# A two-block transformer in fp32 on one core: the second block's layer loop written out, with other hand-overs at its two edges

## The chip, the cores and the metric

The kernel runs on one core of a Trainium2 chip. The metric is the device time of one execution, in microseconds. The core's engines run side by side and hand work over by semaphores: TensorE (PE) multiplies, VectorE (DVE) and ScalarE (ACT) work element by element, SyncE (SP) issues DMA transfers, and ACT issues some too. Each engine takes its own instructions in the order in which they are written.

## The reference

A sequence of 256 tokens with 1024 features goes through two blocks of two layers each. The first block (FFN, Fourier or retention mixer, FFN; modulated norms) ends in a final norm. The second block, which the change touches, is for each layer:

```
for l in range(DEPTH):
    f = _swiglu(_rmsnorm_2(h, ff1_norm_pre[l]), ff1_w_gate[l], ff1_w_up[l], ff1_w_down[l])
    h = h + 0.5 * _rmsnorm_2(f, ff1_norm_post[l])
    m = _hybrid_mixer(_rmsnorm_2(h, mix_norm_pre[l]), w_in[l], conv_w[l], ..., w_out[l])
    h = h + _rmsnorm_2(m, mix_norm_post[l])
    f = _swiglu(_rmsnorm_2(h, ff2_norm_pre[l]), ff2_w_gate[l], ff2_w_up[l], ff2_w_down[l])
    h = h + 0.5 * _rmsnorm_2(f, ff2_norm_post[l])
```

`_rmsnorm_2` divides by the root of the mean square over the features and multiplies by a gain; `_swiglu` is `(silu(h @ wg) * (h @ wu)) @ wd` with 2816 hidden features; the mixer holds a state-space part, a pooling part and attention. All is float32.

## The kernel before

**Layout.** Activations lie transposed: `h` holds 8 tiles of 128 features, each over the tokens (256 in the second block). A float32 product is made of three products in a reduced format: each operand is split into a high part and the rest (`u_hi`, `u_lo`; `w_hi`, `w_lo`; `g_hi`, `g_lo` for the hidden features of an FFN), and PE computes hi x hi, hi x lo and lo x hi (line 779).

**Weights.** Every matrix product (`Gemm`) is a row of units. A unit is a piece of weights, up to 4 tiles of 128 rows by 256 columns (512 KB). SP loads it into one of four slots of `raw` (`sp_gemm`, line 568) as soon as DVE has split the unit that lay there. ACT makes `w_hi` from it when PE has finished the unit of four places before (`split_hi`, line 581), and DVE makes `w_lo` (`split_lo`, line 587). The routine `stream` (line 590) writes the order of ACT and of DVE for a `Gemm`: at each unit u it first splits unit u + 4, and then evicts PSUM if u closes a pair of banks. If there is a next `Gemm` in the same list, its first four units are split within the stream of the current one (`follower`); if there is none, they are not.

**Stages.** `block1()` and `block2(l)` list the stages. Each engine walks through the lists and writes its own part. `first = block1()` is written out. `block2(l)` is written once per engine inside a hardware loop `Fori` over the two layers, so that semaphore counts are values in a register, computed from the layer. A layer is: gain, `up` (11 turns of four units), `down` (2 turns of six units), post norm, norm, the mixer's products and the mixer, `mix_out`, post norm, and again gain, `up`, `down`, post norm. Within `up` and longer products the turns after the first run in an inner `Fori`.

**The norm between two stages.** The last product's squares are summed by ACT and DVE, then over partitions by PE (lines 859, 862); ACT takes the root (841), DVE the reciprocal (850). `dve_post` (line 935) then walks over the eight tiles: `f_out` times `rstd` (943), and the result times the gain added to `h` (948). ACT makes `u_hi` of a tile from `h` and the next gain (893, `act_gain`), and DVE makes `u_lo` (900, `dve_gain_tile`), on which PE waits before the first product with that tile. The next stage's own `rstd` is applied later, behind the product: `up` has `norm_after`, so that a gate pair is evicted with the multiplication by `rstd` (696). When a gain stage follows in the same list, `dve_post` writes `dve_gain_tile` of tile k - 3 between the steps of tile k. This is so behind `mix_out`.

**The two edges.** At the end of the first block DVE multiplies tile by tile (lines 1771, 1772), all eight, and zeroes `poolw` (1774). ACT issues the load of `tables` (1696). At the start of each layer ACT splits the first four units of `up`, waits until all eight tiles are done (`post_ready`), issues four loads of `pool_w` (1708) and one of 8 columns of `w_in` into `dtw` (1709), and copies the layer's small vectors from `lvecs` to `lvec` (1711). Only then does `act_gain` scale the first tile. DVE splits one unit, waits for the copy and writes the gain tiles one behind the other (`dve_gain`). `tables`, `poolw` and `dtw` lie at the start of the memory that the first block's `g_hi` used; all are first read in the mixer.

Of the kernel before, what the change touches and what calls it, by code (L numbers as in the profile page):

```python
# [19 lines left out]
P = 128  # L20
D = 1024
DT = D // P
SEQ = 256
# [3 lines left out]
RING = 4  # L27
# [5 lines left out]
POOL_GROUPS = 4  # L33
ATTN_HEADS, ATTN_DH = 4, 64
LAYERS2 = 2
# [81 lines left out]
class Tally:  # L117
# [11 lines left out]

    def enter(self, layer, stages):  # L130

        self.start, self.per = dict(self.n), {}
        for s in stages:
            for k, v in s.counts().items():
                self.per[k] = self.per.get(k, 0) + v
        for k, v in self.per.items():
            self.n[k] = layer * v + self.start.get(k, 0)

    def leave(self, layers):
        self.n = dict(self.start)  # L140
        for k, v in self.per.items():
            self.n[k] = self[k] + layers * v
# [67 lines left out]
def build(nc, T):  # L210
# [27 lines left out]
    def block1():  # L238
# [51 lines left out]
        out.append(Stage("final", {"post": DT}))  # L290
        return out

    def block2(l):
        w = lambda name: T[name][l]
# [3 lines left out]
        def ffn(n, pre, post):  # L298
            gate, up = w(f"ff{n}_w_gate_2"), w(f"ff{n}_w_up_2")
            pick = lambda it, pair, k0, kt: rows((gate, up)[pair])[:, k0:k0 + kt, bass.ds(it * UCOLS, UCOLS)]  # L300
            return [Stage("gain", {"uhi": DT, "ulo": DT, "sq": 4, "sum": 2}, gain=pre),
# [4 lines left out]
                    stats(SEQ, "gemm", half=True), Stage("post", {"post": DT, "px": DT}, gain=post)]  # L306
        return ffn(1, "pre1", "post1") + [
            stats(SEQ, "post"), Stage("apply", {"xr": DT, "uhi": DT, "ulo": DT}, tokens=SEQ, gain="mix_pre"),
            Gemm("z", 1, [4, 4], in_turn(wi, 0), SEQ, evac="to_z", k_outer=True, waits="ulo"),
            Gemm("xbc", 2, [4, 4], in_turn(wi, 512), SEQ, evac="to_xbc"),  # L310
            Stage("conv", {}),
            Gemm("pool_v", 1, [4, 4], fixed((1544, 2312)), SEQ, mode="tokens", evac="to_pool_v"),
            Stage("steps", {}),
            Gemm("q_k", 1, [4, 4], fixed((1800, 2056)), SEQ, evac="to_q_k"),
            Stage("mixer", {"mix_lo": 3}),
            Gemm("mix_out", 2, [4, 4], in_turn(w("w_out_2")), SEQ, evac="store", waits="mix_lo", k_outer=True,
                 last_half_first=True),
            stats(SEQ, "gemm"), Stage("post", {"post": DT, "px": DT}, gain="mix_post")
# [7 lines left out]
    with ctx:  # L326
# [24 lines left out]
        lvec = sb("lvec", [P, LAYER_N])  # L351
# [28 lines left out]
        tab_spec = [("tables", [P, TWO_N], f32), ("poolw", [P, 2, P], f32), ("dtw", [P, 64], f32)]  # L380
# [26 lines left out]
        def lv(name, a=0, n=1):  # L407
            return lvec[:, LAYER_AT[name] + a:LAYER_AT[name] + a + n]
# [14 lines left out]
        lvec_copied = sem("lvec_copied")  # L423
# [100 lines left out]
        class Order:  # L524
# [5 lines left out]
            def enter(self, layer, per):  # L530
                self.first, self.per, self.n = self.n, per, layer * per + self.n
                self.k = 0

            def leave(self, layers):
                assert self.k == self.per, ("instructions of a layer in order", self.k)
                self.n = self.first + layers * self.per

            def link(self, ins):

                self.n = self.n + 1  # L540
# [1342 lines left out]
```

## Time and profile before

| | |
|---|---|
| device time of three runs | 3221.47, 3224.37, 3224.98 us; median 3224.37 |
| span of the profiled execution, first to last instruction | 3221.9 us |
| time of the profiled execution beside its span | not given separately; the median of the runs is 2.5 us above the span |
| TensorE matmul | busy 2935.3 us, 91% |
| TensorE weight load | 2633.6 us, 82% |
| DVE | 1701.1 us, 53% |
| ACT | 1283.5 us, 40% |
| DMA | 428.43 MB, mean 133 GB/s |
| mean granted TensorE clock | 0.953 of full |

Busy time is how long an engine had an instruction in work. Matmuls are pipelined, so their ends are modelled; their starts and the idle time ahead of them are the safer readings. The idle time ahead of an instruction stands in brackets, with the instruction that released it.

### The profile page before, as it was taken

The numbers are of one execution on the slowest core, as the hardware profiler recorded it, in microseconds if no ns is written. First come the engines' busy times: TensorE is split into PE (matmuls) and PEld (weight loads), VectorE is DVE, ScalarE is ACT, GpSimd is POOL, SyncE is SP. The second block draws the span as 40 slices with busy tenths as digits, with TensorE's granted clock in tenths as the row PEclk, the third lists the DMA queues.
The fourth block names the chain that finished last, engine by engine and source line by source line (L and its number), as shares of the span: only waits on it lengthen the run. The fifth ranks groups of instructions, "written<-read, shape, count | busy, mean of one in ns | idle before, by whom it ended". The sixth has DMA issues, their size and how long they took to land.

```text
span 3221.9 us, 47690 instructions
## 1 busy us (share of the span) xinstructions
PE 2935.3 (91%) x18444; PEld 2633.6 (82%) x18444; DVE 1701.1 (53%) x2287; ACT 1283.5 (40%) x1584; POOL 0.5 (0%) x7
## 2 busy tenths in 40 slices
PE   4999997899998999997997799898888989978898
PEld 3888886688886888886996799798868979977898
DVE  5554455455323553455237555665666656557664
ACT  5443334433223432334232444444434444444443
POOL 0000000000000000000000000000000000000000
PEclk8999998999999999998998899999898989989899
DMA  5454451155322453453340355565324646641464
GB/s 186 144 163 144 132 162 61 53 157 163 98 91 79 143 159 103 137 164 114 94 137 20 105 176 184 166 183 180 108 63 138 181 146 180 186 124 53 131 182 131
DMA packets 428460, 428.43 MB, mean 133 GB/s; under 512 B 16032, under 2 KB 426912, under 8 KB 428192
## 3 DMA queue, kind: packets, MB, share of 16 engines
q1 hardware_dynamic: 424736, 422.63, 43.1%
q10 hardware_dynamic: 3584, 3.90, 0.4%
q8 instruction: 92, 1.51, 0.2%
q14 instruction: 48, 0.39, 0.0%
HBM read 425.43 MB, written 1.05 MB: 132 GB/s over the span
## 4 chain that ended last, share of the span: by engine, by line
PE 86%; DVE 6%; ACT 4%; issue 2%; DMA 1%; ACTq 0%; DVEq 0%; SPq 0%
PE ps L779 72%; PE ps L767 4%; PE ps L753 3%; DVE rstd L850 1%; PE ps L859 1%; PE ps L862 1%; PE ps L1124 1%; DVE w_lo L587 1%; ACT w_hi L581 1%; ACT u_hi L877 1%; DMA raw<-in_w_mod 1%; PE ps L1008 1%; PE ps L1112 1%; DVE h L948 1%; ACT tmp L877 1%
## 5 line engine op out<-in xcount | busy, mean ns | idle before, releaser
L587 DVE TENSOR_TENSOR w_lo<-raw,w_hi 128x1024 fp32r<-128x1024 f32 (+1 forms) x816 | 973.8, 1203 | 1167.7 <-ACT w_hi L581 1151.6
L779 PE MATMUL ps<-u_hi,w_hi 128*128 128x256 f32 (+1 forms) x3648 | 1184.7, 325 | 116.5 <-DVE u_lo L926 50.9
L581 ACT ACTIVATE w_hi<-raw 128x1024 fp32r<-128x1024 f32 (+1 forms) x816 | 837.7, 1038 | 1128.3 <-PE ps L779 1038.2
L779 PE MATMUL ps<-u_lo,w_hi 128*128 128x256 f32 (+1 forms) x3648 | 1173.7, 322 | 0.0
L779 PE MATMUL ps<-u_hi,w_lo 128*128 128x256 f32 (+1 forms) x3648 | 1173.6, 322 | 0.0
L779 PEld LDWEIGHTS ps<-u_hi,w_hi 128*128 128x128 f32 x3648 | 708.8, 194 | 182.9 <-issue 53.1
L779 PEld LDWEIGHTS ps<-u_hi,w_lo 128*128 128x128 f32 x3648 | 708.9, 194 | 48.7
L779 PEld LDWEIGHTS ps<-u_lo,w_hi 128*128 128x128 f32 x3648 | 710.2, 195 | 44.8
L779 PE MATMUL ps<-g_hi,w_hi 128*128 128x256 f32 (+1 forms) x1408 | 451.4, 321 | 0.0
L779 PE MATMUL ps<-g_hi,w_lo 128*128 128x256 f32 (+1 forms) x1408 | 451.2, 320 | 0.0
L779 PE MATMUL ps<-g_lo,w_hi 128*128 128x256 f32 (+1 forms) x1408 | 451.2, 320 | 0.0
L779 PEld LDWEIGHTS ps<-g_hi,w_lo 128*128 128x128 f32 x1408 | 264.1, 188 | 24.3
L779 PEld LDWEIGHTS ps<-g_hi,w_hi 128*128 128x128 f32 x1408 | 264.2, 188 | 22.3
L779 PEld LDWEIGHTS ps<-g_lo,w_hi 128*128 128x128 f32 x1408 | 264.2, 188 | 21.9
L753 PE MATMUL ps<-w_hi,cond_cols 128*128 128x256 f32 x576 | 146.4, 287 | 30.2 <-DVE turned L627 15.9
L660 ACT ACTIVATE g_hi<-tmp 128x512 f32 (+3 forms) x88 | 69.8, 793 | 229.1 <-DVE tmp L708 229.1
L753 PE MATMUL ps<-w_lo,cond_cols 128*128 128x256 f32 x576 | 145.5, 286 | 0.0
L753 PEld LDWEIGHTS ps<-w_hi,cond_cols 128*128 128x128 f32 x576 | 111.5, 194 | 36.2 <-issue 26.5
L713 DVE TENSOR_TENSOR g_lo<-tmp,g_hi 128x512 f32 (+3 forms) x88 | 78.5, 892 | 90.9 <-ACT g_hi L660 90.9
L753 PEld LDWEIGHTS ps<-w_lo,cond_cols 128*128 128x128 f32 x576 | 111.4, 193 | 5.0
L859 PE MATMUL ps<-acc,ones 128*128 128x256 f32 (+1 forms) x76 | 38.3, 644 | 67.7 <-DVE acc L827 45.0
L819 ACT ACTIVATE tmp<-h 128x512 f32<-128x512 f32 (+1 forms) x57 | 42.3, 742 | 139.3 <-DVE h L727 65.9
(222 smaller groups left out, 2041.1 us busy)
## 6 DMA issues: line engine op xcount, KB each, us to landing
raw<-in_ffn_w_in SPq DMA_DIRECT2D x176, 512.0 KB, 3.5
raw<-in_w_mod SPq DMA_DIRECT2D x144, 512.0 KB, 4.5
raw<-in_ff_w_gate SPq DMA_DIRECT2D x88, 512.0 KB, 4.0
raw<-in_ff_w_up SPq DMA_DIRECT2D x88, 512.0 KB, 4.2
raw<-in_ffn_w_out SPq DMA_DIRECT2D x64, 512.0 KB, 3.4
raw<-in_ff_w_down SPq DMA_DIRECT2D x64, 512.0 KB, 4.0
raw<-in_ret_w_in SPq DMA_DIRECT2D x48, 512.0 KB, 3.7
raw<-in_w_in SPq DMA_DIRECT2D x40, 512.0 KB, 3.7
```

The lines of the kernel that those rows point to most:

```text
L581: act.activation(w_hi[:, slot, 0:cols], raw[:, slot, 0:cols], ACT.Copy).then_inc(hi_ready, 1)
L587: dve.tensor_tensor(w_lo[:, slot, 0:cols], raw[:, slot, 0:cols], w_hi[:, slot, 0:cols].bitcast(f32), ALU.subtract).then_inc(lo_ready, 1)
L660: act.activation(hi[:, bass.ds((it + g.first) * 2, 2), 0:g.tokens], tmp2[:, :, 0:g.tokens], ACT.Copy).then_inc(g_hi_ready, 1)
L713: dve.tensor_tensor(lo[:, two, 0:g.tokens], tmp2[:, :, 0:g.tokens], hi[:, two, 0:g.tokens].bitcast(f32), ALU.subtract).then_inc(g_lo_ready, 1)
L753: ins = pe.matmul(ps[:, 4 + pair % 2, 0:UCOLS], cond_cols[:, 4 * (k0 + k):4 * (k0 + k) + P], w[:, slot, k * UCOLS:(k + 1) * UCOLS], start= ...
L767: ins = pe.matmul(out, a, w[:, slot, cols], start=begins and k == 0 and n == 0 and tb % 2 == 0, stop=final and k == kt - 1 and n == 2, ski ...
L779: ins = pe.matmul(out, w[:, slot, cols], a, start=begins and k == 0 and n == 0, stop=final and k == kt - 1 and n == 2)
L819: act.activation(out[:, :, 0:n], source[:, 2 * m:2 * m + 2, 0:n], ACT.Square).then_inc(squares_ready, 1)
L850: dve.reciprocal(rstd[:, 0:n], rstd[:, 0:n]).then_inc(rstd_ready, 1)
L859: pe.matmul(ps[:, STAT, 0:n], ones[:, :], acc[:, i, 0:n], start=i == 0, stop=False)
L862: ins = pe.matmul(ps[:, STAT, 0:n], ones[:, :], tmp1[:, i, 0:n], start=False, stop=i == 1)
L877: ins = act.activation(out[:, tok], tmp2[:, k % 2, tok], ACT.Identity, scale=coef[:, g.more["piece"], k, s:s + 1], bias=mod[:, g.more["pie ...
```

## The change

The layer loop over the second block is replaced by one list of both layers' stages, written out for each engine, so semaphore counts there are constants except in the inner loops. `follower` now sees over both edges (`whole` for the first block's products, `second` for the layers'). At the first edge `dve_final` zeroes `poolw`, then handles norm and gain tiles interleaved as `dve_post` does; at the layer edge `dve_post` finds the gain stage behind it. `lvec`, its copy and its semaphore are gone; `lv(l, ...)` reads `lvecs`. `poolw` and `dtw` hold both layers' data. They and `tables` are loaded once, by SP, in `sp_tables`, between the last tile of the first layer's first `up` and the first tile of its `down`.

```
-        tab_spec = [("tables", [P, TWO_N], f32), ("poolw", [P, 2, P], f32), ("dtw", [P, 64], f32)]
+        tab_spec = [("tables", [P, TWO_N], f32), ("poolw", [P, 2 * LAYERS2, P], f32), ("dtw", [P, LAYERS2, 64], f32)]
...
+        def sp_tables(sp):
+            sp.wait_ge(poolw_zeroed, 1)
+            sp.dma_start(tables[:, :], T["tables2"]).then_inc(tables_landed, 16)
+            for l in range(LAYERS2):
+                sp.dma_start(dtw[:, l, :].rearrange("p (k n) -> p k n", n=8),
+                             rows(T["w_in_2"][l])[:, :, 1536:1544]).then_inc(dtw_landed, 16)
+                for g in range(POOL_GROUPS):
+                    r = slice((g % 2) * 64, (g % 2 + 1) * 64)
+                    sp.dma_start(poolw[r, 2 * l + g // 2, r], T["pool_w_2"][l, g]).then_inc(poolw_landed, 16)
...
+        def dve_final(dve, t, gain):
+            dve.memset(poolw[:, :, :], 0.0).then_inc(poolw_zeroed, 1)
+            dve.wait_ge(lvec_landed, 16)
+            if begun(t["stat"]):
+                dve.wait_ge(rstd_ready, t["stat"])
+            for k in range(DT + 3):
+                if k < DT:
+                    if begun(k - 1):
+                        dve.wait_ge(post_ready, k - 1)
+                    dve.tensor_tensor(tmp2[:, k % 2, 0:SEQ], h[:, k, 0:SEQ], rstd[:, 0:SEQ], ALU.mult
+                                      ).then_inc(post_scaled_ready, 1)
+                if 0 < k <= DT:
+                    dve.wait_ge(post_scaled_ready, k)
+                    dve.tensor_scalar(h[:, k - 1, 0:SEQ], tmp2[:, (k - 1) % 2, 0:SEQ], vecs("final_g", k - 1), None,
+                                      ALU.mult).then_inc(post_ready, 1)
+                if k >= 3:
+                    dve_gain_tile(dve, gain, t, k - 3)
...
+        second = [stage for l in range(LAYERS2) for stage in block2(l)]
+        whole = first + second
...
@@ @block.sync
-            with sp.Fori(0, LAYERS2) as l:
-                stages = block2(l)
...
+            for g in second:
+                if isinstance(g, Gemm):
+                    sp_gemm(sp, g, t)
+                t.add(g)
+                if g is follower(second, -1):
+                    sp_tables(sp)
...
@@ @block.scalar
-                    stream(act, g, t, follower(first, j), split_hi, act_evacuate)
+                    stream(act, g, t, follower(whole, j), split_hi, act_evacuate)
...
-                act.dma_start(tables[:, :], T["tables2"]).then_inc(tables_landed, 16)
-            with act.Fori(0, LAYERS2) as l:
-                for u in range(RING):
-                    split_hi(act, follower(stages, -1), t, 0, u)
-                act.wait_ge(lvec_landed, 16)
-                act.wait_ge(poolw_zeroed, 1)
-                act.wait_ge(post_ready, t["post"])
-                for g in range(POOL_GROUPS):
-                    act.dma_start(poolw[r, g // 2, r], T["pool_w_2"][l, g]).then_inc(poolw_landed, 16)
-                act.dma_start(dtw[:, :].rearrange("p (k n) -> p k n", n=8), ...
-                act.activation(lvec[:, :], lvecs[:, bass.ds(l * LAYER_N, LAYER_N)], ACT.Copy
-                               ).then_inc(lvec_copied, 1)
+            act.wait_ge(lvec_landed, 16)
+            for j, g in enumerate(second):
+                if isinstance(g, Gemm):
+                    stream(act, g, t, follower(second, j), split_hi, act_evacuate)
...
@@ @block.vector
-                split_lo(dve, up, t, 0, 0)
-                dve.wait_ge(lvec_copied, l + 1)
-                        if j == 0:
-                            dve_gain(dve, g, t, {3: [1], 7: [2, 3]}, up)
+                    behind = second[j + 1] if j + 1 < len(second) and second[j + 1].kind == "gain" else None
+                    dve_post(dve, g, t, behind)
```

## Rows read from the trace of the kernel before

**Rows 1.** The page's chain of waits, share by engine.
```profile
PE 86%; DVE 6%; ACT 4%; issue 2%; DMA 1%; ACTq 0%; DVEq 0%; SPq 0%
```

**Rows 2.** Groups by line and form, PE: count | busy us, mean ns | idle before, releasers.
```profile
L779 PE MATMUL ps<-u_hi,w_hi 128*128 128x256 f32 x2464 | 716.1, 291 | 78.2 <-DVE u_lo L900 39.1 <-DVE u_lo L926 23.8 <-ACT tmp L651 5.4
...
L779 PE MATMUL ps<-u_hi,w_lo 128*128 128x256 f32 x2464 | 707.6, 287 | 0.0
...
L779 PE MATMUL ps<-g_hi,w_lo 128*128 128x256 f32 x880 | 242.9, 276 | 0.0
```

**Rows 3.** Timeline, first edge: start us, duration us, instruction [idle before <-releaser].
```profile
2035.36 0.28 PE L779 MATMUL ps<-g_hi,w_lo 128*128 128x256 f32 x1
...
2038.94 1.75 DVE L850 RECIPROCAL rstd<-rstd 128x256 f32<-128x256 f32 x1 [2.39 <-ACT rstd L841]
...
2046.60 0.27 DVE L1774 MEMSET poolw<- 128x256 f32 x1
...
2051.99 0.58 PE L779 MATMUL ps<-u_hi,w_hi 128*128 128x256 f32 x1 [13.58 <-DVE u_lo L900]
...
2066.81 0.68 DVE L696 TENSOR_TENSOR tmp<-ps,rstd 128x512 f32<-128x512 f32 x1
```

**Rows 4.** Timeline, layer edge.
```profile
2621.30 0.28 PE L779 MATMUL ps<-g_hi,w_lo 128*128 128x256 f32 x1
...
2624.77 1.75 DVE L850 RECIPROCAL rstd<-rstd 128x256 f32<-128x256 f32 x1 [2.47 <-ACT rstd L841]
...
2633.49 2.47 ACTq L1708 DMA_DIRECT2D poolw<-in_pool_w  x4
...
2638.22 0.58 PE L779 MATMUL ps<-u_hi,w_hi 128*128 128x256 f32 x1 [14.00 <-DVE u_lo L900]
...
2653.42 0.68 DVE L696 TENSOR_TENSOR tmp<-ps,rstd 128x512 f32<-128x512 f32 x1
```

**Rows 5.** Timeline, inside the layer, behind mix_out.
```profile
2414.92 0.28 PE L779 MATMUL ps<-u_hi,w_lo 128*128 128x256 f32 x1
...
2422.53 1.75 DVE L850 RECIPROCAL rstd<-rstd 128x256 f32<-128x256 f32 x1 [3.78 <-ACT rstd L841]
...
2427.72 0.58 PE L779 MATMUL ps<-u_hi,w_hi 128*128 128x256 f32 x1 [5.74 <-DVE u_lo L900]
...
2444.72 0.68 DVE L696 TENSOR_TENSOR tmp<-ps,rstd 128x512 f32<-128x512 f32 x1
```

**Rows 6.** Timeline and one window, behind the first layer's first down.
```profile
2243.40 0.28 PE L779 MATMUL ps<-g_hi,w_lo 128*128 128x256 f32 x1
...
2244.80 1.23 DVE L587 TENSOR_TENSOR w_lo<-raw,w_hi 128x1024 fp32r<-128x1024 f32 x1 [0.81 <-ACT w_hi L581]
...
2250.83 1.75 DVE L850 RECIPROCAL rstd<-rstd 128x256 f32<-128x256 f32 x1 [3.60 <-ACT rstd L841]
...
core 0: us, PE busy (x) PEld busy (x) DVE busy (x) ACT busy (x) POOL busy (x), PEclk, DMA share, GB/s
2243.40:2250.83 7.43, 3.88 (x11) 2.60 (x9) 3.02 (x4) 2.16 (x3) 0.00 (x0) 0.77 0.70 210
```

**Rows 7.** Timeline, first up to first down: SP, ACT, PE.
```profile
2163.16 0.37 SPq L568 DMA_DIRECT2D raw<-in_ff_w_up  x1
...
2167.56 0.37 SPq L568 DMA_DIRECT2D raw<-in_ff_w_down  x1
...
2176.75 1.04 ACT L581 ACTIVATE w_hi<-raw 128x1024 fp32r<-128x1024 f32 x1
...
2183.66 0.29 PE L779 MATMUL ps<-g_hi,w_hi 128*128 128x256 f32 x1
```

**Rows 8.** DMA issues: count, KB each, median us from issue to landing.
```profile
tables<-in_tables ACTq DMA_DIRECT2D x1, 1920.0 KB, 7.2
...
poolw<-in_pool_w ACTq DMA_DIRECT2D x8, 16.0 KB, 2.0
```

**Rows 9.** Timeline, nine linked small instructions, layer loop and first block.
```profile
2329.91 1.85 DVE L977 SCALAR_TENSOR_TENSOR small<-small 128x16 f32<-128x16 f32 x9
...
1516.86 1.77 DVE L977 SCALAR_TENSOR_TENSOR lgam<-lgam 128x8 f32<-128x8 f32 x9
```

More of the change, by code:

```diff
@@ L128, in add @@
             self.n[k] = self[k] + v
[L130 to L142, printed above, removed]
 def loop(eng, a, b, body):
@@ L289, in block1 @@
         out.append(stats(SEQ, "gemm"))
-        out.append(Stage("final", {"post": DT}))
+        out.append(Stage("final", {"post": DT, "px": DT}))
         return out
     def block2(l):
+        of_layer = lambda kind, counts: Stage(kind, counts, layer=l)
         w = lambda name: T[name][l]
@@ L350, in build @@
         lvecs = sb("lvecs", [P, LAYERS2 * LAYER_N])
-        lvec = sb("lvec", [P, LAYER_N])
         mod = sb("mod", [P, 3, 24, 2])
@@ L528, in __init__ @@
                 self.eng, self.sem, self.n = eng, sem, 0
[L530 to L536, printed above, removed]
             def link(self, ins):
                 self.n = self.n + 1
-                self.k = self.k + 1 if hasattr(self, "k") else 0
                 ins.then_inc(self.sem, 1)
@@ L880, in act_apply_tile @@
                 else:
-                    ins = act.activation(out[:, 0:n], tmp2[:, k % 2, 0:n], ACT.Copy, scale=lv(g.more["gain"], k))
+                    ins = act.activation(out[:, 0:n], tmp2[:, k % 2, 0:n], ACT.Copy, scale=lv(*g.more["gain"], k))
             ins.then_inc(u_hi_ready, 1)
@@ L892, in act_gain @@
                     act.wait_ge(post_ready, t["post"] - DT + k + 1)
-                act.activation(u_hi[:, k, 0:SEQ], h[:, k, 0:SEQ], ACT.Copy, scale=lv(g.more["gain"], k)
+                act.activation(u_hi[:, k, 0:SEQ], h[:, k, 0:SEQ], ACT.Copy, scale=lv(*g.more["gain"], k)
                                ).then_inc(u_hi_ready, 1)
@@ L899, in dve_gain_tile @@
             dve.wait_ge(u_hi_ready, t["uhi"] + k + 1)
-            dve.scalar_tensor_tensor(u_lo[:, k, 0:SEQ], h[:, k, 0:SEQ], lv(g.more["gain"], k),
+            dve.scalar_tensor_tensor(u_lo[:, k, 0:SEQ], h[:, k, 0:SEQ], lv(*g.more["gain"], k),
                                      u_hi[:, k, 0:SEQ].bitcast(f32), ALU.mult, ALU.subtract
@@ L904, in dve_gain_tile @@
                 dve_add_squares(dve, SEQ, k // 2, t)
-        def dve_gain(dve, g, t, units_after, gemm):
-            for k in range(DT):
-                dve_gain_tile(dve, g, t, k)
-                for u in units_after.get(k, []):
-                    split_lo(dve, gemm, t, 0, u)
         def dve_scaled(dve, g, t, k):
@@ L1748, in _ @@
                 if isinstance(g, Gemm):
-                    stream(dve, g, t, follower(first, j), split_lo, dve_evacuate, dve_turn_rows)
+                    stream(dve, g, t, follower(whole, j), split_lo, dve_evacuate, dve_turn_rows)
                 elif g.kind == "squares":
@@ new lines, in _ @@
+                    dve_final(dve, t, second[0])
+                t.add(g)
+            for j, g in enumerate(second):
+                if isinstance(g, Gemm):
+                    if g.norm_after:
+                        dve_stats(dve, stats(g.tokens, "gemm"), t)
+                    stream(dve, g, t, follower(second, j), split_lo, dve_evacuate, dve_turn_rows)
+                elif g.kind == "stats":
+                    dve_stats(dve, g, t)
+                elif g.kind == "apply":
+                    dve_apply(dve, g, t)
+                elif g.kind == "post":
+                    behind = second[j + 1] if j + 1 < len(second) and second[j + 1].kind == "gain" else None
+                    dve_post(dve, g, t, behind)
+                elif g.kind == "conv":
+                    dve_conv(dve, t, g.more["layer"], order)
+                elif g.kind == "steps":
+                    dve_steps(dve, g.more["layer"], order)
+                elif g.kind == "mixer":
+                    dve_mixer(dve, g.more["layer"], order)
+                t.add(g)
```

156 lines of the change are left out of this document (51 added, 105 removed).

## The prediction

> **What bounds the kernel now.** The chain of waits comes first: TensorE (PE) holds 86% of it, VectorE (DVE) 6% [rows 1]. A change to the other engines counts only where PE stands still. The groups by line and form come next: behind its 2464 first matmuls on `u_hi` stand 78.2 us of idle time, of which 39.1 end on `u_lo L900` [rows 2]. These waits are few and long, so the timeline is the third view. PE stops for 13.58 us between the first block and the second [rows 3] and for 14.00 us between the two layers [rows 4]. These are the two edges that the change rewrites. Inside a layer the same norm already hands over tile by tile: behind `mix_out`, PE waits 5.74 us for the same first `u_lo` tile [rows 5]. That seam and the one behind the first `down` [rows 6] show what the edges become, because they run the code that the edges get.
>
> I measure each edge between two points that lie on PE's path: the start of the last matmul of the old stage, and the first `L696`, which evicts the first gate pair of `up`. From there the loops of `up` run alike. Before: first edge 2066.81 - 2035.36 = 31.45 us [rows 3], layer edge 2653.42 - 2621.30 = 32.12 us [rows 4].
>
> **Hand-over tile by tile (removes).** Today DVE finishes all eight tiles of the norm, then ScalarE (ACT) issues four `pool_w` loads (2.47 us [rows 4]), one `dtw` load and the copy of `lvec`, and only then scales the first tile. In the change DVE interleaves the gain tiles three behind the norm, and ACT has no loads there. From the start of the reciprocal to the first `L696` that is 27.87 us at the first edge [rows 3], 28.65 us at the layer edge [rows 4] and 22.19 us inside the layer [rows 5]. Gains: 5.68 and 6.46 us, 12.14 us together. The branch back of the layer loop lies inside the 28.65 us and goes with it.
>
> **Look-ahead over the edge (adds, on the path).** `stream` of the last `down` now has a follower, so ACT and DVE split the first four units of `up` inside it. The split of the fourth unit needs the slot that the last unit of `down` frees. It therefore starts when PE is done, and in both queues it stands ahead of the last eviction: behind it wait the squares sum, the copy out of PSUM, the last squares and the stat matmuls. Today the edges have none of this: last matmul to reciprocal is 2038.94 - 2035.36 = 3.58 us [rows 3] and 3.47 us [rows 4]. The first `down` of the layer, which has a follower, shows it: ACT's split, then DVE's (1.23 us from 2244.80, though the last matmul began at 2243.40), and the reciprocal at 2250.83, 7.43 us after that matmul [rows 6]. `mix_out` needs 7.61 us [rows 5]. TensorE's granted clock over those 7.43 us is 0.77 on average, so part of the stretch ran at the 1.2 GHz level; the stall ahead of the stat matmuls is part of the price. I take 7.43, as the stage before both edges is a `down`.
>
> Layer edge after: 7.43 + 22.19 = 29.62 us, against 32.12: **-2.50 us**. First edge after: 7.43 + 22.19, plus 0.11 because its eviction with residual is slower (3.58 against 3.47), plus the zeroing of `poolw`. That memset is twice as wide now and stands between the reciprocal and the first norm tile. The half-width one took 0.27 us [rows 3]; the wide one lies between that and 0.54, I take 0.4. Sum 30.13 us against 31.45: **-1.32 us**. That the final norm only multiplies where the post norm also adds to `h` I leave at nothing. The two edges together: **-3.8 us**. With 7.61 for 7.43 at both it would be -3.5, and if the look-ahead delayed nothing it would be 12.14 - 0.4 = -11.7. The measured seam is the nearest row, and I keep -11.7 for the range.
>
> **Tables on the weight queue (moves).** SyncE (SP) issues `tables`, two `dtw` and eight `poolw` loads right behind the last tile of the first `up`, ahead of the first tile of `down`. SP's last `up` tile goes out at 2163.16 and the first `down` tile at 2167.56 [rows 7]. ACT's four `poolw` issues took 2.47 us [rows 4], 0.62 each; eleven such are 6.8 us, so the first `down` tile leaves at about 2170.3, 2.8 us late. Its data stand behind the transfers: 7.2 us for the 1920 KB of `tables` [rows 8], at that rate 1.9 us for the `up` tile ahead of it and 1.9 us for its own 512 KB, and for ten small loads, mostly overlapped, an estimated 2 us. It lands at 2163.2 + 13.0 = 2176.2. ACT wants it at 2176.75, and PE only at 2183.66 [rows 7], after a split by ACT and one by DVE that take about 2.3 us. What hides the loads is thus PE's 20 us of work on tiles that came before them. **Cost 0**; without that cover it would be the 9.2 us of other loads that stand ahead of the tile. From above: if each of the ten small loads held the queue for its full 2.0 us [rows 8], the tile would land at 2163.2 + 11.0 + 20 = 2194.2 and PE would stand for 2194.2 + 2.3 - 2183.66 = 12.8 us. Below zero nothing is to be had here: the loads that leave ACT are already counted at the edges.
>
> **Layer loop written out, per-layer constants, `lvec` gone.** Waits against a register become waits against a constant, and small operands come from `lvecs` in place. The nine linked instructions of `L977` took 1.85 us inside the layer loop, on 16 columns, and 1.77 us in the first block, with constants and on 8 columns [rows 9]. At most 0.08 us in nine waits could be the register, and I expect none. PE waits in a row of its own only at the seams above. Cost and gain **0**. As PE covers the rest of both layers, a hidden saving on ACT or DVE moves nothing; only the edges count.
>
> **Sum.** Edges -3.8, tables 0, loop 0. Against the profiled span of 3221.9 us that is 3218.1 us. The median of the runs is 3224.37 us, 2.5 us above that span, and the same difference makes **3220.6 us**, or -0.12%. About 0.2% (6.4 us) is what a measurement of this kernel can tell from no change, so I forecast no change that counts. Own range of this case: -2 to -6 us, 3218 to 3222.5.
>
> **Rivals.**
> - *The look-ahead delays nothing.* If the last splits fell in time ahead of the eviction, the edges would give 11.7 us: 3212.7 us. For it: the reciprocal-to-`L696` rows alone promise that much. Against: both seams with a follower show over 7.4 us from last matmul to reciprocal, both without one under 3.6 [rows 3 to 6]. Chance 0.12.
> - *The tables starve the ring (slower).* Small loads held one behind another in the SP queue make the first `down` tile late for PE. It decides once the tile lands after 2183.66 - 2.3 = 2181.4, 5.2 us later than I take, and makes the kernel slower than before 3.8 us beyond that. At the bound worked out above: -3.8 + 12.8, 3233.4 us. For it: the loads stood in ACT's queue, in a stretch in which PE was idle; now they stand in the queue of the tiles, at full demand. Against: the slack. Chance 0.06. By the Trainium skill (DMA: Bandwidth & Descriptors, "Queues, rings and completion order") a DMA engine takes the descriptors of one queue's ring in order, but changes between the rings of different queues packet by packet. That speaks against the move: on ACT's ring the weights could pass the tables, on SP's they can't. No row here shows two such loads on one ring.
> - *Placement (slower).* `lvec` (456 bytes) lay ahead of the `g` tiles, and `poolw` and `dtw` grow ahead of the second block's. PE's 256-column matmuls on `g` tiles take 276 ns, those on `u` tiles 287 [rows 2]. Only the latter run in part at the half clock, behind the seams; I take 7 of the 11 ns as pace. Nothing in the profile says why, so it may hang on the address. If `g` fell to the pace of `u`, that is 3 x 880 matmuls x 7 ns = 18.5 us: 3220.6 + 18.5 = 3239.1 us. Against: the tiles of the first and the second block lie at different addresses and keep one mean. Chance 0.07. The same cause could speed up others; with what else I don't see, 0.05 for a gain of some 10 us.
> - *The edge doesn't pipeline.* If the gain tiles waited for the whole norm, as now, each edge would lose ACT's loads (2.47 us and up) and pay 7.43 - 3.47 = 3.96 for the look-ahead: up to 3.0 us for both, 3227 us at most. The order of the code inside the layer speaks against it. Chance 0.04.
>
> **How the numbers follow.** The forecast has 0.66. Faster by over 0.2%: 0.12 + 0.05 and 0.09 of my own case, where both edges give more than I count: 0.26. Slower by over 0.2%: 0.06 + 0.07 less what stays small: 0.11. Within: 0.63. The range takes in the first rival and the spread of the runs before (3221.47 to 3224.98), and leaves out the two slow rivals and the far end of the fast one: 3212 to 3226.5.
>
> **What would show it.** Right: at both edges a split of 1.2 us on DVE directly ahead of the last eviction, the reciprocal 7.3 to 7.7 us after the last matmul, PE's wait for the first `u_lo` near 5.7 us instead of 14, and reciprocal to first `L696` near 22.2 us. ACT's wait for a raw tile at the start of the first `down` under 1 us and no PE wait there. `g` matmuls still at 276 ns. Wrong: the reciprocal under 5 us after the last matmul, PE idle at the start of the first `down`, other means for L779, or a stage away from the edges that changes its length by more than 1 us.

## The result, and the profile after

The changed kernel takes 3236.3 us (median of 7 runs, 3233.6 to 3239.4), the kernel before 3224.4 us beside it: ratio 1.0035, 95% interval 1.0025 to 1.0044. I had forecast 3220.6 us. The change makes the kernel slower by 12 us, and the time lies near the rival "placement", which I had given 0.07.

The page of the changed kernel shows the same bound as [rows 1]. Its groups by line and form answer to [rows 2]; L767 is now the line of the GEMM matmuls.

```profile
PE 86%; DVE 7%; ACT 4%; issue 2%; DMA 1%; SPq 0%; ACTq 0%; DVEq 0%
```

```profile
L767 PE MATMUL ps<-u_hi,w_hi 128*128 128x256 f32 x2464 | 718.5, 292 | 62.3 <-DVE u_lo L908 23.8 <-DVE u_lo L888 22.9 <-ACT tmp L639 5.1
...
L767 PE MATMUL ps<-u_hi,w_lo 128*128 128x256 f32 x2464 | 709.0, 288 | 0.0
...
L767 PE MATMUL ps<-g_hi,w_lo 128*128 128x256 f32 x880 | 247.3, 281 | 0.0
```

The idle time ahead of `u_hi` fell from 78.2 to 62.3 us: the change did what it says, though not all of that reaches the total, as the look-ahead puts part of it back ahead of the statistics. But the matmuls on `g` with 256 columns went from 276 to 281 ns, three groups of 880, 242.9 to 247.3 us each: 13.2 us. These run back to back, so here that is time on the path. One down stage shows it by its starts. The rows give count, duration min/median/max, and the first and last start; first the kernel before, then the changed one, the same stage.

```profile
L779 PE MATMUL ps<-g_hi,w_hi x176: 276/276/286, 1975.6 to 2035.1; 128*128 128x256 f32 x176
```

```profile
L767 PE MATMUL ps<-g_hi,w_hi x176: 276/281/286, 1981.0 to 2043.1; 128*128 128x256 f32 x176
```

59.5 us became 62.1 us: 113.4 ns from start to start became 118.3 (59.5 / 525 and 62.1 / 525: the row holds every third matmul, and from its first to its last start there are 525 steps). All five down stages with 256 columns show the same, 5 x 2.6 = 13.0 us.

The first edge, for [rows 3]:

```profile
2043.35 0.28 PE L767 MATMUL ps<-g_hi,w_lo 128*128 128x256 f32 x1
...
2044.82 1.23 DVE L575 TENSOR_TENSOR w_lo<-raw,w_hi 128x1024 fp32r<-128x1024 f32 x1 [0.90 <-ACT w_hi L569]
2045.96 0.68 DVE L815 TENSOR_TENSOR acc<-acc,tmp 128x512 f32<-128x512 f32 x1
...
2050.43 1.75 DVE L838 RECIPROCAL rstd<-rstd 128x256 f32<-128x256 f32 x1 [3.00 <-ACT rstd L829]
2052.24 0.48 DVE L939 MEMSET poolw<- 128x512 f32 x1
...
2055.58 0.55 PE L767 MATMUL ps<-u_hi,w_hi 128*128 128x256 f32 x1 [5.69 <-DVE u_lo L888]
...
2072.31 0.68 DVE L684 TENSOR_TENSOR tmp<-ps,rstd 128x512 f32<-128x512 f32 x1
```

And the layer edge, for [rows 4]:

```profile
2629.94 0.28 PE L767 MATMUL ps<-g_hi,w_lo 128*128 128x256 f32 x1
...
2631.41 1.23 DVE L575 TENSOR_TENSOR w_lo<-raw,w_hi 128x1024 fp32r<-128x1024 f32 x1 [0.90 <-ACT w_hi L569]
...
2637.67 1.75 DVE L838 RECIPROCAL rstd<-rstd 128x256 f32<-128x256 f32 x1 [3.84 <-ACT rstd L829]
...
2642.86 0.55 PE L767 MATMUL ps<-u_hi,w_hi 128*128 128x256 f32 x1 [5.73 <-DVE u_lo L888]
...
2659.74 0.68 DVE L684 TENSOR_TENSOR tmp<-ps,rstd 128x512 f32<-128x512 f32 x1
```

From the last matmul to the first gate eviction: 2072.31 - 2043.35 = 28.96 us (before 31.45) and 2659.74 - 2629.94 = 29.80 us (before 32.12). The edges give 4.8 us, and I had forecast 3.8. Each step of the forecast is there: DVE's split of 1.2 us ahead of the eviction, the reciprocal 7.08 and 7.73 us after the last matmul, 5.7 us of wait for the first `u_lo` tile.

A third difference lies far from the change, at 632 us. Windows of both kernels, the column after POOL being the granted clock:

```profile
632.00:638.00 6.00, 4.70 (x19) 3.57 (x20) 3.97 (x7) 6.00 (x14) 0.00 (x0) 0.99 0.00 0
```

```profile
632.00:638.00 6.00, 5.53 (x12) 3.94 (x13) 3.98 (x8) 6.00 (x13) 0.00 (x0) 0.50 0.00 0
```

In the changed kernel TensorE stays at 1.2 GHz (a granted clock of 0.50) some 6 us longer behind the same waits. From the norm's reciprocal at 621 us to the next one at 1033 us the kernel before takes 1033.57 - 621.35 = 412.22 us, the changed one 1036.86 - 621.21 = 415.65: 3.4 us more. The sum of the three, 13.0 - 4.8 + 3.4 = 11.6 us, is nearly all of the 12.4 us between the two profiled spans.

### The profile page after: what moved, and what is told of

It reads as the page before. It is cut to its first block, busy times and chain, and to the rows that moved or that the text cites. A ratio compares the mean times of both kernels' runs of the same rounds, so it can differ in the third digit from the quotient of the medians.

```text
span 3234.3 us, 46336 instructions
## 1 busy us (share of the span) xinstructions
PE 2957.5 (91%) x18444; PEld 2652.8 (82%) x18444; DVE 1699.8 (53%) x2287; ACT 1285.1 (40%) x1582; POOL 0.5 (0%) x7
## 3 DMA queue, kind: packets, MB, share of 16 engines
q1 hardware_dynamic: 427600, 424.79, 43.4%
## 4 chain that ended last, share of the span: by engine, by line
PE 86%; DVE 7%; ACT 4%; issue 2%; DMA 1%; SPq 0%; ACTq 0%; DVEq 0%
PE ps L767 73%; PE ps L741 3%; PE ps L755 3%; DVE rstd L838 1%; PE ps L1125 1%; ACT w_hi L569 1%; PE ps L850 1%; DVE w_lo L575 1%; PE ps L847 1%; ACT u_hi L865 1%; DMA raw<-in_w_mod 1%; PE ps L1009 1%; ACT tmp L865 1%; DVE tmp L925 1%; DVE h L930 1%
## 5 line engine op out<-in xcount | busy, mean ns | idle before, releaser
L767 PE MATMUL ps<-u_hi,w_hi 128*128 128x256 f32 (+1 forms) x3648 | 1188.8, 326 | 99.8 <-DVE u_lo L908 50.2
L767 PE MATMUL ps<-u_lo,w_hi 128*128 128x256 f32 (+1 forms) x3648 | 1177.3, 323 | 0.0
L767 PE MATMUL ps<-u_hi,w_lo 128*128 128x256 f32 (+1 forms) x3648 | 1176.7, 323 | 0.0
L767 PEld LDWEIGHTS ps<-u_hi,w_hi 128*128 128x128 f32 x3648 | 710.9, 195 | 169.3 <-issue 89.8
L767 PEld LDWEIGHTS ps<-u_hi,w_lo 128*128 128x128 f32 x3648 | 711.5, 195 | 48.4
L767 PEld LDWEIGHTS ps<-u_lo,w_hi 128*128 128x128 f32 x3648 | 712.9, 195 | 44.8
L767 PE MATMUL ps<-g_lo,w_hi 128*128 128x256 f32 (+1 forms) x1408 | 456.2, 324 | 0.0
L767 PE MATMUL ps<-g_hi,w_lo 128*128 128x256 f32 (+1 forms) x1408 | 456.1, 324 | 0.0
L767 PE MATMUL ps<-g_hi,w_hi 128*128 128x256 f32 (+1 forms) x1408 | 456.1, 324 | 0.0
L767 PEld LDWEIGHTS ps<-g_hi,w_lo 128*128 128x128 f32 x1408 | 265.1, 188 | 23.7
L767 PEld LDWEIGHTS ps<-g_lo,w_hi 128*128 128x128 f32 x1408 | 265.1, 188 | 21.9
L767 PEld LDWEIGHTS ps<-g_hi,w_hi 128*128 128x128 f32 x1408 | 265.1, 188 | 21.8
```

The costliest lines, as they stand in the source:

```text
L767: ins = pe.matmul(out, w[:, slot, cols], a, start=begins and k == 0 and n == 0, stop=final and k == kt - 1 and n == 2)
```

## The experiments

**a1_align: the old addresses back.** A byte address below is that in a partition's memory, as the compiler assigned it. The `g` tiles started at 133952 before and start at 133472 in the changed kernel, because `lvec` (480 bytes with padding) is gone. The second block's `g` tiles stood at 150592 and stand at 151392: there the growth of `poolw` and `dtw`, 1024 + 256 = 1280 bytes, comes on top, a multiple of 256.

```
         lvecs = sb("lvecs", [P, LAYERS2 * LAYER_N])
+        pad = sb("pad", [P, 120])
```

> The changed kernel with a dead buffer of 480 bytes per partition where lvec lay, nothing else. The g tiles of both blocks then start 64 bytes past a multiple of 128 again, as in the kernel before; in the changed kernel they start 96 past. Placement theory: the starts of the 256-column matmuls on g tiles stand 113.4 ns apart again instead of 118.3 in all five such down stages, 5 x 528 x 4.9 ns = 12.9 us, so 3236.3 - 12.9 = 3223.4 us, and 3220 where TensorE gets the full clock in the seam at 628 us as early as in the profile of before. Rival, the written-out loop or the look-ahead is what costs: 118.3 ns stay, 3236 us.

Measured: 3217.9 us (12 runs), ratio to the kernel before 0.9983, interval 0.9974 to 0.9991. The same stage as above:

```profile
L768 PE MATMUL ps<-g_hi,w_hi x176: 276/276/286, 1975.1 to 2034.6; 128*128 128x256 f32 x176
```

59.5 us again, and in all five stages. 480 dead bytes take 18.4 us off the medians; 13.0 of them are this pace, and another 3.4 between the two profiles is the late clock at 632 us, which this profile doesn't have. Without the placement the change is faster than the kernel before, by 6.9 us, more than my 3.8.

**a2_before_pad32: the placement alone.**

```
         eps = sb("eps", [P, 2])
+        pad = sb("pad", [P, 8])
```

> The kernel before with 32 dead bytes per partition ahead of the g tiles, nothing else: they start 96 bytes past a multiple of 128 instead of 64. Placement theory: 118.3 ns between the 256-column matmuls on g tiles instead of 113.4, no other stage moves, 3224.4 + 12.9 = 3237.3 us. Rival, placement costs nothing and the difference is in the change's code: 113.4 ns stay, 3224 us.

Measured: 3240.5 us (5 runs), ratio 1.0049, interval 1.0036 to 1.0062. The same stage:

```profile
L780 PE MATMUL ps<-g_hi,w_hi x176: 277/281/285, 1978.0 to 2040.2; 128*128 128x256 f32 x176
```

62.2 us, and all five stages run so. Nothing of the change is in this kernel, and it is slower than the changed one by about what the edges give. (Of its 15.7 us, 13 are this pace; the rest is not broken down.) Together with a1_align this shows the cause from both sides.

**a3_late_split: the fourth split off the path.**

```
-                    elif nxt is not None:
+                    elif nxt is not None and not (g.squares and u == g.units - 1):
                         split(eng, nxt, t_next, 0, v - g.units)
...
+            split_late(split_hi)      # ACT: behind the root in act_stats
...
+            split_late(split)         # DVE: first thing in stream of the next GEMM
```

> a1_align, and in addition the fourth look-ahead split of every stage that ends in a residual or a store is taken out of the stage: ACT issues it behind the root of the statistics, DVE ahead of the next GEMM's loop. That holds at both rewritten edges and at nine seams inside the blocks. My step (the fourth split stands ahead of the last eviction and costs 7.43 - 3.5 = 3.9 us): reciprocal 3.5 us after the last matmul at each such seam, 11 seams x up to 3.9 us = up to 43 us less than a1_align; with 512 tokens less, so 20 to 43 us. Rival, the split is hidden and the 7.43 us are the eviction's own: no change against a1_align. Rival, the fourth unit now comes late for TensorE: the reciprocals are early and the time comes back as idle time ahead of the fourth unit.

Measured: 3191.7 us (4 runs), ratio 0.9893, interval 0.9879 to 0.9908: 26 us under a1_align. The first edge of its trace:

```profile
2020.31 1.23 DVE L576 TENSOR_TENSOR w_lo<-raw,w_hi 128x1024 fp32r<-128x1024 f32 x1 [0.82 <-ACT w_hi L570]
...
2020.88 0.28 PE L777 MATMUL ps<-g_hi,w_lo 128*128 128x256 f32 x1
...
2025.17 1.05 ACT L570 ACTIVATE w_hi<-raw 128x1024 fp32r<-128x1024 f32 x1
2025.31 1.75 DVE L849 RECIPROCAL rstd<-rstd 128x256 f32<-128x256 f32 x1 [2.39 <-ACT rstd L839]
```

The fourth split is now the ACT row at 2025.17, beside DVE's reciprocal. The reciprocal comes 4.43 us after the last matmul, against 2042.29 - 2034.88 = 7.41 in a1_align; the third split still ends behind the last matmul, the likely reason why it is not 3.5. So the look-ahead's price, 7.43 - 3.5, was read rightly, and 3.0 of the 3.9 us can be had back up to the reciprocal. Of that TensorE loses some behind the seam: at four seams it waits some 0.6 us for a split. The 26 us are 2.4 us for each of the 11 seams.

**b3_edge_late: the first rival of the prediction made true.** As a3_late_split, at the two rewritten edges alone (`nxt.more.get("edge")` in the condition).

> a1_align with the late fourth split at the two rewritten edges alone. This is the rival of the prediction in which the look-ahead delays nothing, made true: against a1_align 2 x 3.3 us less (a3_late_split lost 3.32 us at the first edge and 1.85 at the second between the marks of the two profiles), 3217.9 - 5.2 to 6.6 = 3211 to 3213 us. Rival, at the edges the splits are covered and all of a3's 26 us come from the seams inside the blocks: 3218.

Measured: 3217.9 us (11 runs), ratio 0.9979, interval 0.9970 to 0.9988; a1_align had 0.9983. The forecast was too high. It counted 3.32 and 1.85 us for the two edges of a3_late_split, but between this document's two points they took 2048.35 - 2020.88 = 27.47 and 2625.22 - 2597.51 = 27.71 us, 3.5 under a1_align in all. Here too, the two edges take 2065.31 - 2038.56 = 26.75 and 2647.17 - 2618.75 = 28.42 us, against 29.70 and 28.97 in a1_align, so 3.5 us come out at them, not 5.2 to 6.6, while the runs of either kernel spread over 8 to 11 us. No difference is shown. At the layer edge only 0.55 us are left, though the first product starts 9.44 us after the last matmul and not 12.42. Two windows of 4 us, each from 4 us after that product, first in a1_align, then here, show where part of it goes:

```profile
2633.56:2637.56 4.00, 4.00 (x29) 4.00 (x29) 3.15 (x8) 2.15 (x4) 0.00 (x0) 0.79 0.00 0
```

```profile
2632.19:2636.19 4.00, 4.00 (x21) 4.00 (x21) 3.15 (x8) 2.15 (x4) 0.00 (x0) 0.50 0.00 0
```

The granted clock stays at its lower level longer, 21 matmuls start in the window and not 29, and behind it TensorE waits 0.56 us for a split. With one profile of each kernel, how much of this is the edit's and how much the execution's is not shown.

**b2_after_again: is the late clock the change's?** The changed kernel, unchanged.

> The changed kernel once more, unchanged, for a second profile. Its first profile lost 3.4 us against the kernel before in the seam at 628 us, where the full clock came at 638.6 instead of 632.5 us with the same work ahead of it. Theory, that is the lot of an execution: the second profile has the full clock near 632.5 at that place, or another such place moves. Rival, it belongs to the changed kernel: 638.6 again.

Measured: 3234.0 us, one run. The same place:

```profile
632.00:638.00 6.00, 6.00 (x18) 4.75 (x19) 3.60 (x6) 6.00 (x13) 0.00 (x0) 0.63 0.00 0
```

This profile is late again, by 3.4 us from reciprocal to reciprocal (1034.46 - 618.87 = 415.59 us). But b3_edge_late, whose instructions up to 2000 us are a1_align's, has 0.61 in this window and 3.3 us too, while a1_align has 1.00 and nothing. So it is not tied to the placement or to the change's code; whether the changed kernel draws it more often isn't settled. The Trainium skill (TensorE: Matmul & The Clock Gate, Part 1) says of the rise of the clock that it is "run-variable"; these traces agree.

**d2_tables_gpsimd: what the tables cost on SP.** In the changed kernel SP's row of the first up to the first down, for [rows 7] (start, duration, instruction, count):

```profile
2166.30 2.65 SPq L545 DMA_DIRECT2D raw<-in_ff_w_up  x2
2169.16 0.35 SPq L553 DMA_DIRECT2D tables<-in_tables  x1
2169.57 0.43 SPq L555 DMA_DIRECT2D dtw<-in_w_in  x1
2170.03 5.78 SPq L559 DMA_DIRECT2D poolw<-in_pool_w  x4
2175.85 0.59 SPq L555 DMA_DIRECT2D dtw<-in_w_in  x1
2176.48 2.95 SPq L559 DMA_DIRECT2D poolw<-in_pool_w  x4
2179.47 12.58 SPq L545 DMA_DIRECT2D raw<-in_ff_w_down  x8
```

Eleven issues take 10.3 us, not my 6.8. ACT then waits 0.88 and 0.43 us for raw tiles, and TensorE not at all:

```profile
2183.14 1.06 ACT L569 ACTIVATE w_hi<-raw 128x1024 fp32r<-128x1024 f32 x1 [0.88 <-DMA raw<-in_ff_w_down]
2184.64 1.06 ACT L569 ACTIVATE w_hi<-raw 128x1024 fp32r<-128x1024 f32 x1 [0.43 <-DMA raw<-in_ff_w_down]
```

The edit of the run, on a1_align:

```
-                if g is follower(second, -1):
-                    sp_tables(sp)
...
+            sp_tables(pool)
```

> a1_align with the eleven loads of tables, dtw and poolw issued by GpSimd as soon as poolw is zeroed, at the edge, and none on SP. It tests the prediction's step that the tables cost nothing on the weight queue. My step (hidden by 20 us of TensorE's work): no change against a1_align, 3218 us, and the first down of the layer starts no earlier. Rival, the tables do hold the weight ring back: up to 12.8 us less, 3205 us. If they come to lie in the way of the first up's weights at the edge, it is slower than a1_align.

Measured: 3220.2 us (11 runs), ratio 0.9987, interval 0.9978 to 0.9996. No gain is shown (a1_align had 0.9983): the step "cost 0" holds.

**a4_bench and b1_bench_addresses: matmuls alone, on zeros.**

```
for j, (w, x) in enumerate(((wh, hi), (wh, lo), (wl, hi))):
    ins = mm(out, at(w + w0, P), at(x + x0, n), k == 0 and j == 0, k == 3 and j == 2)
```

> Matmuls alone, on zeros, no work of the kernel in it: runs of 96 in the kernel's pattern (weights hi, hi, lo; moving hi, lo, hi), one line of code for each placement. The moving tiles start 0, 32, 64 or 96 bytes (and 16, 48, 80) past a multiple of 128, with 256 or 512 columns; the weights at 0, 32 or 64. Theory, the start of the moving tile sets the pace: with 256 columns 120 ns at 0 (as the u tiles, which start at 0), 118.3 at 96, 113.4 at 64; with 512 columns 226.7 at 0 and 233 at 64 and 96. Rival, something else in the stages makes the pace (the transfers and the other engines beside them, the distance of the two halves): one spacing for all placements of a size.

Measured: 117 to 119 ns from start to start for all seven starts of the moving tile with 256 columns; 231 to 233 with 512. The theory, that the tile's own start sets the pace, fell. In this bench the high and the low halves happened to stand 128 bytes apart modulo 256, so no line had one distance for all its matmuls; the second bench has.

> Matmuls alone again, on zeros, no work of the kernel in it, but every operand at the byte address that it has in the kernel (one buffer over the partition), with the kernel's loops over the two halves of the columns and four inner tiles; one line of code for each placement. In the first bench no start of the moving tile gave the 113.4 ns of the g tiles: 117.8 to 118.8 for all. Theory 1, what counts is where the two moving halves and the two weight halves stand relative to each other: the addresses of the g tiles before give 113.4, those after 118.3, those of the u tiles 120, with nothing running beside; moving u by 64 bytes shows whether it can be had for u too. Theory 2, the other engines and the transfers make the difference: all near 118.

Measured, one row for each placement (96 matmuls, first and last start):

```profile
L72 PE MATMUL ps<-X x96: 281/281/281, 105.0 to 116.2; 128*128 128x256 f32 x96
...
L74 PE MATMUL ps<-X x96: 280/283/283, 127.7 to 139.1; 128*128 128x256 f32 x96
L75 PE MATMUL ps<-X x96: 276/276/286, 139.2 to 150.0; 128*128 128x256 f32 x96
L76 PE MATMUL ps<-X x96: 277/280/285, 150.1 to 161.3; 128*128 128x256 f32 x96
...
L86 PE MATMUL ps<-X x96: 279/279/283, 262.8 to 274.0; 128*128 128x256 f32 x96
...
L92 PE MATMUL ps<-X x96: 279/284/285, 331.3 to 342.7; 128*128 128x256 f32 x96
L93 PE MATMUL ps<-X x96: 276/276/284, 342.8 to 353.6; 128*128 128x256 f32 x96
...
L98 PE MATMUL ps<-X x96: 389/389/397, 399.2 to 420.7; 128*128 128x512 f32 x96
L99 PE MATMUL ps<-X x96: 394/394/394, 421.0 to 443.1; 128*128 128x512 f32 x96
...
L107 PE MATMUL ps<-X x96: 276/276/285, 555.0 to 565.8; 128*128 128x256 f32 x96
```

The span over 95 is the pace, good to 1 ns, as starts are given to 0.1 us. Write d for the start of the moving tile less that of the weights, modulo 256. L74 has the addresses of `u` (d = 0): 120.0 ns. L75 has those of the second block's `g` before (d = -64): 113.7. L76 has those after (d = -32): 117.9. L86 is `u` 64 bytes further (d = 64): 117.9; L92 is the old `g` with the weights 64 further (d = 128): 120.0. L93 is `u` with the weights 64 further (d = -64): 113.7. The other distances stand in the last section. So no other engine and no transfer is needed for the difference, and both operands count. One pair doesn't fit a fixed pace for each distance: L72 and L107 have the same addresses, those of the first block's `g` before (d = -64), and took 117.9 and 113.7 ns. f2_u192_again comes back to this. With 512 columns the order turns round: d = 0 (L98) 226.3 ns, d = -64 (L99) 232.6.

**e1_after_pad32: the rule tried on g.**

```
         eps = sb("eps", [P, 2])
+        pad = sb("pad", [P, 8])
```

> The changed kernel with 32 dead bytes per partition ahead of the g tiles, for its trace: g then starts where u does, at distance 0 from the weights modulo 256. If the distance is what counts, the 256-column matmuls on g tiles start 120 ns apart, as those on u do, neither 118.3 as in the changed kernel nor 113.4 as in the kernel before; 5 x 528 x 1.7 ns = 4.5 us more than the changed kernel, 3238 to 3241 us. Rival, any place but the old one gives 118.3; or a round multiple of 128 gives the fast pace back, 3223 us.

Measured: 3229.5 us, one run. A stage with 256 columns, and one with 512:

```profile
L768 PE MATMUL ps<-g_hi,w_hi x176: 283/283/283, 1969.9 to 2032.9; 128*128 128x256 f32 x176
...
L768 PE MATMUL ps<-g_hi,w_hi x176: 389/389/389, 897.7 to 1016.7; 128*128 128x512 f32 x176
```

63.0 / 525 = 120.0 ns in all five, as the rule says. I forgot its other half for the sum: with 512 columns the pace went from 233 (the changed kernel: 903.7 to 1026.2, 122.5 us) to 227 ns (119.0 us), 3.5 us in this stage. The first of the three such stages became shorter by 2.5 us (144.1 to 141.6), the third by about as much, some 8.5 us together. 3236.3 + 4.5 - 8.5 = 3232.3 us; the one run took 3229.5, and the 2.8 us between are not explained.

**c1_weights64, c2_u64, d1_u192, f1_all_distances: using it.** All on a3_late_split. The first moves the weights by 64 bytes; the others move `u` from the retention norm on, by a view that starts 16 or 48 columns further. In c2 the buffers also grow by 128 bytes, so that the two halves of `u` stand at +64 and -64; in d1 and f1 they grow by 256, and both halves stand at -64. f1 moves wide `g` tiles too, and zeroes `poolw` ahead of the reciprocal:

```
+        wpad = sb("wpad", [P, 16])                    # c1
...
+            u_hi.first = u_lo.first = 16 if (...) else 0   # c2; d1: 48
...
+            u_hi.first = u_lo.first = g_hi.first = g_lo.first = 48 if (...) else 0   # f1
-        g_hi, g_lo = overlay([("g_hi", [P, FT, NTOK], f32r), ...])
+        g_hi, g_lo = [Moved(None, t, FT) for t in overlay([("g_hi", [P, FT * NTOK + 64], f32r), ...])]
```

> a3_late_split with 64 dead bytes per partition ahead of the two weight halves. They and the g tiles behind them move by 64 bytes, u stays: g keeps its distance to the weights, u changes it from 0 to 64 (mod 128). In the second bench the addresses of u gave 120.0 ns with 256 columns and 113.7 once the weights stood 64 bytes further; with 512 columns 226.3 and 233.7. Theory, the distance between the moving tile and the weights (mod 128) sets the pace: the stages on u with 256 columns fall from 120.0 to 113.5 ns between starts, (3 x 2464 + 960) x 6.4 ns = 54 us, where TensorE never waits at half pace; the stages on u with 512 columns rise from 226.8 to 233, 3 x 1184 x 6.5 ns = 23 us; g stays at 113.4. 3191.7 - 54 + 23 = 3161 us, and 3175 if a third of the gain lies beside waits. Rival, the start address of the moving tile alone counts: u stays at 120, g goes to another pace, 3192 to 3215 us.

> a3_late_split with u 64 bytes further from the retention norm on, that is for nearly all stages with 256 columns, and at its old place for those with 512; the weights stay. Same theory as for c1_weights64 without its loss: 3191.7 - 50 = 3142 us, 3155 if part lies beside waits; starts 113.5 ns apart in the GEMMs on u from 1500 us on. In the bench u moved by 64 gave 117.9 instead of 113.7, so half the gain, 3170, is possible too. Rival as there: no change, 3192.

> c2_u64 with u moved by 192 bytes instead of 64, and the two halves of u 65 x 256 bytes long, so that both stand alike. The g tiles of the kernel before stand 64 bytes short of the weights, counted modulo 256, and so do all lines of the second bench with 113.7 ns, while a distance of 0 gave 120, 128 gave 118.9 to 120, and 64, 32 and 96 gave 117.9. Theory, the distance modulo 256 counts and 192 (that is -64) is the fast one: u goes from 120.0 to 113.4 ns in every stage with 256 columns from 1480 us on, which c2_u64 reached only in the token stages (its two halves stood at +64 and -64): 3191.7 - (7392 + 960) x 6.6 ns = 3137 us, 3150 if part lies beside waits. Rival, the distance is only half of it and a stage falls into one pace or another by chance, as c1_weights64 showed with the same distances (113.4 ns in some stages, 117.8 in others): 3155 to 3180 us.

> d1_u192 with the wide g tiles treated as u is: at distance 0 from the weights (modulo 256) in the three down stages with 512 columns, at -64 in the last one with 256; the second block's g stays at -64; and the zeroing of poolw stands ahead of the reciprocal instead of behind it. Theory: in e1_after_pad32 the 512-column matmuls on g went from 233 to 227 ns at distance 0, so 3 x 528 x 3 x 6.5 / 3 ns = 10 us, and 0.5 us for the zeroing: 3165 - 10.5 = 3155 us, clearly under d1_u192. Rival, the 512-column stages gain nothing in this setting, or stages with 256 columns fall to 117.8 ns by chance as often as before and cover it: 3155 to 3165 us without order.

Measured: c1 3182.7 us (0.9842, 0.9816 to 0.9869), c2 3180.7 (0.9857, 0.9841 to 0.9874), d1 3165.1 (0.9811, 0.9797 to 0.9824), f1 3157.4 (0.9786, 0.9768 to 0.9804). Each is faster than a3_late_split, by the ratios, and c1, c2 and d1 give less than the rule promised. d1 gained 27 us of the 55 counted, 37 in its profile: some stages ran at 117.8 ns though they stand at d = -64. In c2 the low half of `u` stands at d = 128 in the early stages, and these got slower besides: 192 matmuls with 512 columns, back to back, took 44.6 us where a3_late_split took 43.4. f1 has the 512-column stage below at 227 ns (119.0 us for 525 steps) and the lowest median of the study, 67 us under the kernel before, though its interval and d1's overlap:

```profile
L791 PE MATMUL ps<-g_hi,w_hi x176: 389/389/390, 891.1 to 1010.1; 128*128 128x512 f32 x176
```

**f2_u192_again: what picks the pace at d = -64.**

> d1_u192 unchanged, for a second profile: in the first one the five down stages with 256 columns, all at distance -64, ran at 117.8, 113.6, 113.3, 113.3 and 113.3 ns, and the retention stages on u at 117.8. Theory, addresses fix the possible paces, and which of 113.4 or 117.8 a stage takes is fixed by the program's order: the same stages are slow again. Rival, it is drawn in each execution: other stages, or none or all.

Measured: 3169.0 us, one run. The first layer's second down stage, in d1_u192 and in its repeat:

```profile
L790 PE MATMUL ps<-g_hi,w_hi x176: 276/276/276, 2518.3 to 2577.8; 128*128 128x256 f32 x176
```

```profile
L790 PE MATMUL ps<-g_hi,w_hi x176: 280/281/282, 2521.6 to 2583.4; 128*128 128x256 f32 x176
```

59.5 and 61.8 us: the same program at the same addresses, 113.4 ns in one execution and 117.8 in the other. The up and down stages of one run of matmuls mostly share the pace. So at d = -64 the pace is partly drawn in the execution, as L72 and L107 of the bench had it within one. What it hangs on stays open. Where `u` stands at d = 0, every down stage at d = -64 ran at 113.4 ns: 25 of 25, in the profiles of before, a1, a3, b3 and d2.

## Why the prediction was wrong, point by point

**The step that failed** is "Layer loop written out, per-layer constants, `lvec` gone", whose cost and gain the sum put at 0. Taking away a buffer of 456 bytes moved the `g` tiles from d = -64 to d = -32, and that slowed 2640 matmuls by 4.9 ns each: 13.0 us, shown from both sides by a1_align and a2_before_pad32. The prediction had this as a rival, with the right place and sign. It gave 3239.1 us against 3236.3 measured, but that closeness is partly luck. It took 7 ns, the way to the pace of `u` (120.0 - 113.4 = 6.6 by the starts), and `g` went to 118.3 only. With 4.9 ns it would have said 3233.5, and the late clock of 3.4 us, which it didn't have, makes up the difference. Its chance of 0.07 was too low. I argued against it that the tiles of both blocks "lie at different addresses and keep one mean". They do, but at the same distance from the weights modulo 256, and I didn't work the addresses out, though the sizes of the buffers were all in the code.

**The edges** were read rightly: 4.8 us against 3.8 (a1_align: 4.9). Both parts are there, the hand-over tile by tile and the look-ahead that takes most of it back. The first edge gave more (2.5 against 1.3). Its reciprocal came 7.08 us after the last matmul where the sum had 7.54 (7.43 + 0.11). From the reciprocal on it took 21.88 us where the sum had 22.59: the zeroing took 0.48 us, not 0.4, so the other 21.40 us are 0.79 less than [rows 5]. That the final norm only multiplies, which I left at nothing, may be why; no run shows it. At the layer edge it is 22.07 us against 22.19.

**The look-ahead's price** was right in kind: a3_late_split moves one split per seam and gains 26 us. The rival that it delays nothing is refuted by the traces. That the same price stood at nine more seams, I did not say. Of the 26 us of a3_late_split 3.5 come out at the two edges and the other 22 or so at these, against the 4.8 us that the whole change gives at both edges.

**The tables** cost nothing, as forecast, but with less room: the first down tile leaves SP at 2179.5, 10.3 us after the first table, and TensorE takes up that down stage at 2189.1. I put its landing at 2176.2; ACT got it at 2183.14, 3.7 us after its issue, and the median of such tiles is 3.5. So ACT's two short waits come from the late issue. The rule of the Trainium skill that I set against the move (order within a ring) had no part in the tile's delay: `tables`, issued at 2169.16, took 9.0 us to land and was through before the tile left SP. The `dtw` loads on that ring took 6.0 us to land (median) where they took 2.7 on ACT's before, which agrees with the rule but doesn't show it.

**The clock** took 3.4 us at a place that the change doesn't touch. It appears in an unchanged stretch of b3_edge_late as well, so I count it as chance of the execution.

**TensorE inside the layers.** "As PE covers the rest of both layers" was read too widely: in the first layer's mixer, from 2340 to 2391 us of the kernel before, PE is busy for 41.03 of 51 us, so a saving on ACT or DVE could have counted there. The three differences above leave 0.8 us of the total open, so none of any size came out.

With the placement undone the kernel runs in 3217.9 us, 2.7 us under my forecast, just below that case's own range of 3218 to 3222.5.

## What to carry to other kernels

A buffer taken away or resized moves all buffers behind it: work out the start of each tile that TensorE reads before and after, and its distance from the weights modulo 256. Where a matrix product is bound by TensorE, some 4% of its time hung on that here (113.4 against 118.3 ns), which outweighed a whole reordering. A look-ahead whose last step needs what the stage's last step frees is better placed behind the stage's statistics than ahead of its last eviction: here that gave 26 us.

## What the runs showed of the hardware

The pace of matmuls with separate weight loads depends on where moving tile and weights lie relative to each other. With 256 columns of float32r (the reduced format of the split halves): 120.0 ns at d = 0 and at 96, 118.9 or 120.0 at 128, 117.8 to 118.3 at 32, 64, -96 and -32, and 113.4 to 113.7 or 117.8 to 117.9 at -64. With 512 columns: 226.3 to 226.7 ns at 0, 228.4 at 64, 232.6 at 128, 232.6 to 233.7 at -64, 233 at -32. The Trainium skill (SBUF — State Buffer, "Who interferes with whom") gives TensorE two read ports, for the moving operand and the weight load, "independent", and says that it never waits on anyone. The bench, in which nothing else runs, is hard to square with that: the place of one operand relative to the other is worth up to 6.3 ns per matmul (120.0 against 113.7). Through what they meet no run shows. The Trainium skill's page TensorE: Matmul & The Clock Gate ("Back-to-back issue gap") gives N/2.4 + 2.5 ns as the gap of an isolated matmul, by estimate 109.2 ns for 256 columns and 215.8 for 512, and says that a stream of weight loads and matmuls is faster than this at 512, about 131 ns. It names no format. No stream here is as fast as either, 113.4 and 226.3 being the best.
